# Tokens of the first two experts picked on TensorE instead of gathered by DMA

## The chip, the cores and the metric

The kernel runs on one core of a Trainium2 chip. The metric is the device time in microseconds (us) of one execution; lower is better.

## What is computed

A hybrid decoder layer over 512 tokens and 16 meta tokens: two attention groups, one output projection, and then a hierarchical mixture of experts. The part that matters here is the mixture: each token takes the best of 4 groups and the best 2 of the group's 8 experts, and each of the 32 experts is a SwiGLU of 1024 to 256 to 1024.

```python
u = rmsnorm(h, g_ffn).reshape(B * L, D)
group_logits = (u @ w_group + b_group)
g_idx = jnp.argmax(group_logits, axis=-1)
...
within = jnp.einsum('tg,tge->te', one_hot(g_idx, N_GROUPS), exp_logits)
top_v, top_i = lax.top_k(within, TOP_K)
...
for e in range(N_EXPERTS):
    hid = jax.nn.silu(u @ w1[e]) * (u @ w3[e])
    y = y + combine[:, e:e + 1] * (hid @ w2[e])
return h + y.reshape(B, L, D)
```

## The kernel before

All engines run their own instruction lists, written by hand in program order and tied by semaphores; no scheduler reorders them. The program has a projection stage, two attention sweeps (the second ends near 338 us of the span), an output projection with the router, and the expert loop, which begins near 383 us.

**Router and tables.** The 512 tokens are four tiles `x[:, i, :]` of 128 tokens by 1024 values in SBUF; after `add_mla` (L1462) a tile holds the residual h. For each tile in `TILE_ORDER` (3, 2, 1, 0; the last is `LAST`) PE turns it (L1947) and multiplies by the router's weights (L1959); DVE finds groups and experts (`choose_group`, `choose_experts`, L1482 to L1515) and writes `ehots`, one-hot over 32 experts for each of the two choices; PE counts each token's rank inside its expert (`ranks`, L1970 and L1971); and DVE (`positions`, L1531 to L1540) writes `slot_hot`, one-hot over the expert's 64 slots. `index` (L2130) multiplies `slot_hot` by `tok_hot` on PE and so gives, for each expert and slot, the number of the token in it. DVE turns that into `idx` (L1677), the list of an indirect DMA. A count of tokens for each expert (L2142, L1680, L1681) gives `over`, which is 1 when an expert has more than 64 tokens; a fallback then runs at the end. `keep_warm` (L1793) issues bf16 products whose result nobody reads.

**Expert loop.** ACT has stored each h tile to `h_rows` in DRAM (L1055). For each expert e, POOL issues an indirect DMA (L865) that gathers its rows from `h_rows` into `xg[e % 2]`, 64 rows of 1024 values; rows of empty slots are not written, and so `xg` was zeroed once before (L842). PE turns `xg` by 8 transposes (`turn_gathered`, L2149); DVE scales the result into `xt` (`dve_turned`, L1698); PE multiplies by w1 and w3 (`expand`, L2190); ACT scales rows and copies (L1226); PE turns the hidden rows (L2204); ACT and DVE form the gated product; PE multiplies by w2 (`contract`, L2219); ACT copies (L1248) and POOL scatters the rows to `y_rows` (L855) for the first 29 experts.

**Weights.** An expert's weights are 3 MB (w1, w3 and w2 of 1 MB each). SP issues all loads on one queue into a ring of 7 places. Experts 0 to 5 and w1 of expert 6 are loaded before the loop as memory comes free (the last of them, w1 and w3 of expert 4 and all of expert 5, at the end of the output projection); w3 of expert 6 (L654) waits for the first two gathers (`xg_in`), and its w2 (L675) for `tables_read`, early in the loop. From expert 7 on, w1 and w3 are issued (L660, L661) when `expand` of the expert 7 earlier has ended (`h13_done`) and w2 (L667) when its `contract` has ended. After the last expert the kernel reads `y_rows` back (L696), adds, and stores the output (L699).

## Time and profile before

| | us |
|---|---|
| median of 3 runs | 641.33 |
| lowest and highest | 639.18, 642.98 |
| the profiled execution's own time | 639.66 |
| its span, first to last instruction | 637.8 |
| mean granted TensorE clock | 0.972 of 2.4 GHz |

The profile is of one execution. The span is 1.9 us shorter than that execution's own time, which is 1.7 us under the median. A line such as L2190 is one of kernel.py. "PE" is matmul and "PEld" is the load of the stationary operand, which overlaps it. A float32 product with a stationary table of full width stands as two records, so that "x12" at L2279 are six products. In a timeline the first number is the start in us of the span, the second the length from the first record's start to the last one's end.

### The profile page before, as it was taken

Reading aid. Unit: us, or ns where it says so; the run is one execution under the profiler, and the core shown is the slowest. Engines: PE = TensorE matmul, PEld = TensorE weight load, DVE = VectorE, ACT = ScalarE, POOL = GpSimd, SP = SyncE. Lnnn points to the kernel's source line nnn. Section 1 sums busy time; section 2 is a strip of 40 time slices with the busy share of each in tenths; the row PEclk is TensorE's granted clock in tenths of the full one; section 3 lists DMA queues with packets and bytes.
Section 4 is the critical chain, followed back from the end, with each engine's and each line's share of the span. In section 5 each row is a group of like instructions: output and inputs, shape, how many; then the busy total and the mean of one; then the engine's idle time right before and its main releaser. Section 6 shows DMA issues by size and latency. Waiting matters only on the chain.

```text
span 637.8 us, 9266 instructions
## 1 busy us (share of the span) xinstructions
PE 601.4 (94%) x3595; PEld 412.1 (65%) x3595; DVE 246.5 (39%) x574; ACT 228.6 (36%) x434; POOL 137.9 (22%) x226
## 2 busy tenths in 40 slices
PE   8799999998999997999999989999999999877896
PEld 8588778895666564566788746665665665544554
DVE  3644254224553875287554741111111111101217
ACT  6726414343545353684525611212122122111220
POOL 8100001110133321133400011323323322122110
PEclk8799799999999998999999979999999999899999
DMA  8920000007000064000579488999999999999995
GB/s 251 388 77 1 0 2 0 1 1 282 0 2 0 23 242 141 1 1 1 228 288 409 161 326 292 380 380 393 397 382 391 387 387 394 396 384 400 398 384 209
DMA packets 32525, 139.97 MB, mean 219 GB/s; under 512 B 8681, under 2 KB 10777, under 8 KB 19425
## 3 DMA queue, kind: packets, MB, share of 16 engines
q1 hardware_dynamic: 25440, 124.92, 50.8%
q0 software_dynamic: 6464, 12.36, 5.8%
q10 hardware_dynamic: 576, 2.10, 0.8%
q8 instruction: 29, 0.48, 0.3%
q14 instruction: 16, 0.12, 0.1%
HBM read 131.28 MB, written 16.06 MB: 231 GB/s over the span
## 4 chain that ended last, share of the span: by engine, by line
PE 82%; DVE 10%; issue 3%; DMA 2%; ACT 2%; SPq 0%; DVEq 0%; ACTq 0%
PE ps L2190 18%; PE ps L1857 15%; PE ps L2219 9%; PE ps L2044 5%; PE ps L1933 5%; PE ps L1988 5%; PE ps L2149 5%; PE ps L2033 5%; PE ps L1793 3%; PE ps L2204 2%; DMA w_in_ffcq<-in_w_in 2%; PE ps L2008 2%; PE ps L1830 1%; PE ps L2083 1%; DVE sums_s L1607 1%
## 5 line engine op out<-in xcount | busy, mean ns | idle before, releaser
L2190 PE MATMUL ps<-w,xt 128*64 128x256 f32 x1024 | 118.1, 384 | 13.6 <-issue 12.8
L2190 PEld LDWEIGHTS ps<-w,xt 128*64 128x64 f32 x1024 | 77.5, 139 | 60.9 <-issue 31.9
L1698 DVE TENSOR_TENSOR xt<-ps,g_ffn_c 128x512 f32<-128x512 f32 x32 | 22.1, 691 | 198.7 <-PE ps L2149 198.7
L2219 PE MATMUL ps<-w,hT 128*64 128x512 f32 x256 | 61.8, 605 | 0.0
L1226 ACT ACTIVATE hsb<-ps,row_scale 128x256 f32<-128x256 f32 x32 | 15.1, 473 | 125.2 <-PE ps L2190 125.2
L865 POOL DMA_INDIRECT xg<-h_rows,idx x32 | 30.6, 956 | 113.5 <-PE ps L2149 106.7
L855 POOL DMA_INDIRECT y_rows<-yh,idy x29 | 29.4, 1012 | 64.2 <-ACT yh L1248 64.2
L791 POOL TENSOR_SCALAR_AFFINE_SELECT probT<-probT 128x128 f32<-128x128 f32 (+2 forms) x80 | 23.4, 310 | 90.4 <-ACT probT L1146 89.7
L2044 PE MATMUL ps<-probT,vals 128*128 128x512 f32 (+4 forms) x160 | 42.6, 411 | 0.0
L2033 PE MATMUL ps<-qT,kT 68*128 68x400 f32 (+9 forms) x160 | 42.1, 407 | 0.0
L2149 PEld LDWEIGHTS ps<-ident,xg 64*128 64x128 f32 x256 | 30.6, 200 | 12.4 <-issue 12.4
L1618 DVE TENSOR_REDUCE nmax<-ps 128x1 bf16<-128x528 f32 (+1 forms) x64 | 28.0, 502 | 25.3 <-PE ps L2009 25.3
L2033 PEld LDWEIGHTS ps<-qT,kT 68*128 68x128 f32 (+1 forms) x160 | 26.9, 190 | 14.2 <-issue 7.7
L2044 PEld LDWEIGHTS ps<-probT,vals 128*128 128x128 f32 x160 | 26.8, 191 | 13.9 <-issue 7.1
L1607 DVE RECIPROCAL sums_s<-sums_s 128x512 f32<-128x512 f32 x8 | 26.8, 3352 | 21.6 <-ACT mixT L1156 21.6
L2149 PE MATMUL ps<-ident,xg 64*128 64x64 f32 x256 | 35.0, 277 | 0.0
L1248 ACT ACTIVATE yh<-ps 128x512 f32<-128x512 f32 x29 | 17.3, 597 | 46.4 <-PE ps L2219 46.4
L2219 PEld LDWEIGHTS ps<-w,hT 128*64 128x64 f32 x256 | 15.6, 136 | 22.6 <-issue 18.8
L1146 ACT ACTIVATE probT<-ps 128x416 f32<-128x416 f32 (+1 forms) x48 | 25.1, 540 | 4.6 <-PE ps L2033 4.4
L1793 PE MATMUL ps<-onesb,identb 128*128 128x512 bf16 x91 | 25.5, 428 | 0.8 <-DVE over L1681 0.8
L768 POOL CAST kTb<-kT 68x1024 bf16<-68x1024 f32 (+1 forms) x5 | 4.4, 885 | 97.6 <-PE ps L1857 85.4
L1155 ACT ACTIVATE sums_s<-ps 64x512 f32<-64x512 f32 x16 | 9.5, 591 | 37.8 <-PE ps L2044 37.8
(333 smaller groups left out, 987.5 us busy)
## 6 DMA issues: line engine op xcount, KB each, us to landing
w<-in_w SPq DMA_DIRECT2D x96, 1024.0 KB, 28.4
y_rows<-zeros POOLq DMA_DIRECT2D x1, 4096.0 KB, 12.3
yg<-y_rows SPq DMA_DIRECT2D x4, 1024.0 KB, 11.6
x<-in_x SPq DMA_DIRECT2D x4, 512.0 KB, 5.6
w_in_v<-in_w_in SPq DMA_DIRECT2D x1, 2048.0 KB, 10.5
w_in_k<-in_w_in SPq DMA_DIRECT2D x1, 2048.0 KB, 16.2
w_in_q<-in_w_in SPq DMA_DIRECT2D x1, 2048.0 KB, 21.0
w_oa<-in_w_o SPq DMA_DIRECT2D x1, 2048.0 KB, 10.2
```

The costliest lines, as they stand in the source:

```text
L855: pool.indirect_dma_start(out=y_halves, out_offset=bass.IndirectOffsetOnAxis(ap=idy[:, e:e + 1].bitcast(U32), axis=0), in_=yh[e % 2][:, :] ...
L865: pool.indirect_dma_start(out=xg[e % 2][:, :, :].rearrange("p k n -> p (k n)"), out_offset=None, in_=h_rows, in_offset=bass.IndirectOffset ...
L1607: dve.reciprocal(sums_s[m % 2][:, :], sums_s[m % 2][:, :]).then_inc(sums_inv, 1)
L1793: pe.matmul(ps[:, bank, :], identb[:, :], onesb[:, :].unsqueeze(1).to_broadcast([P, 4, P]), start=True, stop=True)
L1857: ins = pe.matmul(ps[0:unit_rows(u), n % 4, 0:w], ua[:, k, unit_cols(u)], wa[b][:, k, 0:w], start=(k == 0 and p == 0), stop=(k == DK - 1 a ...
L1933: ins = pe.matmul(ps[:, bank + q, :], m[:, k, i * P:(i + 1) * P], w[:, k, q * 512:(q + 1) * 512], start=(n == 0 and k == 0), stop=(n == 2 ...
L1988: ins = pe.matmul(ps[:, b0 + j, 0:nn], src[:, k, block_cols(t) if kind == "kv" else cols(t)], w[:, k, j * nn:(j + 1) * nn], start=(k == 0) ...
L2033: ins = pe.matmul(ps[:, b, c0:c0 + wide], kT[0:depth(g), h, block_cols(j)], qT[0:depth(g), h, q0:], start=True, stop=True)
L2044: ins = pe.matmul(ps[:, OUT, q0:SEQ], value(j, g % H), probT[g % 2][:, b, c0:c0 + SEQ - q0], start=(j == 0), stop=(j == 3))
L2149: ins = pe.transpose(ps[:, b, k * slots:(k + 1) * slots], src[:, k::DK], ident[half, half])
L2190: ins = pe.matmul(ps[j * slots:(j + 1) * slots, 2 + b, 0:F], xt[b][:, k, :], w13[s][:, j, k, :], start=(k == 0), stop=(k == DK - 1))
L2219: ins = pe.matmul(ps[q * slots:(q + 1) * slots, 6 + b, :], hT[b][:, m, :], w2s[s][:, m, q * 512:(q + 1) * 512], start=(m == 0), stop=(m == ...
```

## The change

Experts 0 and 1 are no longer gathered by DMA. `first_slots` makes, for each token tile, a one-hot table of 128 tokens by 2 x 64 slots: `slot_hot` of both choices times `ehots` of experts 0 and 1, and the two choices added. POOL makes it for the first three tiles and DVE for the last. `first_tokens` multiplies each table (stationary) by the tile of h (moving, two halves of 512 columns) and sums over the four tiles in PSUM banks 0 and 1. ACT copies the one half and DVE the other into `xg_both`, the buffer that the gathers of experts 0 and 1 filled. The zeroing of `xg` goes, since every row is now written. The gathers begin with expert 2. Two `keep_warm` calls (10 and 26 products) go. `turn_gathered(1)` and `dve_turned(1)` move ahead of `expand(0)`; PE's wait for `over_made` moves to `turn_hidden(0)`, and DVE's work on `over` behind `dve_turned(1)`. SP no longer waits for the first two gathers ahead of L654's load. Some private semaphores are replaced by the engine's common step semaphore with the same waits.

```diff
+        def first_slots(eng, p):
+            i = TILE_ORDER[p]
+            eng.wait_ge(hot_made, p + 1)
+            if p:
+                eng.wait_ge(first_made, p)
+            eng.tensor_tensor(first_both[:, :, :].rearrange("p c (e s) -> p c e s", e=2),
+                              slot_hot[:, i, :, :].rearrange("p c (e s) -> p c e s", e=2),
+                              ehots[:, i, :, 0:2].unsqueeze(3).to_broadcast([P, 2, 2, slots]), ALU.mult
+                              ).then_inc(first_part, 1)
+            eng.wait_ge(first_part, p + 1)
+            eng.tensor_tensor(first_hot[:, i, :], first_both[:, 0, :], first_both[:, 1, :], ALU.add
+                              ).then_inc(first_made, 1)
@@ SP
-            for b in range(2):
-                sp.wait_ge(xg_in[b], 16)
             sp.dma_start(w13[6][:, 1, :, :], w3_v[6]).then_inc(w13_in[6], 16)
@@ POOL
-            pool.wait_ge(wo_done, 2 * NT)
-            pool.wait_ge(logits_done, NT)
-            pool.memset(xg_both[:, :, :], 0.0).then_inc(xg_blank, 1)
-            pool.wait_ge(xg_blank, 1)
+            for p in range(LAST):
+                first_slots(pool, p)
...
-            for e in range(NE):
-                if e >= 2:
-
-                    pool.wait_ge(xt_done, e - 1)
+            for e in range(2, NE):
+                pool.wait_ge(xt_done, e - 1)
@@ ACT
+            act.wait_ge(first_done, 1)
+            act.activation(first_half(0), ps[:, 0, :], ACT.Copy).then_inc(first_copied, 1)
@@ DVE
             positions(LAST)
+            first_slots(dve, LAST)
+            dve.wait_ge(first_done, 2)
+            dve.tensor_copy(first_half(1), ps[:, 1, :]).then_inc(first_copied, 1)
...
+            dve_turned(0)
+            dve_turned(1)
             dve.wait_ge(counted, 1)
@@ PE
+            def first_tokens(p):
+                i = TILE_ORDER[p]
+                pe.wait_ge(h_made, NT)
+                pe.wait_ge(first_made, p + 1)
+                for q in range(2):
+                    ins = pe.matmul(ps[:, q, :], first_hot[:, i, :], x[:, i, q * 512:(q + 1) * 512],
+                                    start=(p == 0), stop=(p == LAST))
+                    if p == LAST:
+                        ins.then_inc(first_done, 1)
...
-            for p in range(LAST):
-                index(p)
-            keep_warm(COUNT, 10)
+            index(0)
+            index(1)
+            first_tokens(0)
+            first_tokens(1)
             ranks(LAST)
+            first_tokens(2)
+            first_tokens(LAST)
+            index(2)
             index(LAST).then_inc(idx_done, 1)
...
-            pe.wait_ge(over_made, 1)
-            keep_warm(7, 26)
             turn_gathered(0)
+            turn_gathered(1)
             for e in range(NE):
                 expand(e)
-                if e < NE - 1:
+                if 1 <= e < NE - 1:
                     turn_gathered(e + 1)
```

On PE, between the router's last product and expert 1's, the kernel before issues these in a row (`x4` or the like is a count of equal ones; the names are those of the section on the kernel; lines are of the kernel before):

```order
L2130 MATMUL ps<-tok_hot,slot_hot 128x64
L1793 MATMUL ps<-onesb,identb 128x512 x10
L1970 MATMUL ps<-picks,onesb 128x32 [waits pos_made,picks_made]
L1970 MATMUL ps<-picks,onesb 128x32 x2
L1971 MATMUL ps<-picks,before 128x32
L2130 MATMUL ps<-tok_hot,slot_hot 128x64 [waits hot_made]
L2130 MATMUL ps<-tok_hot,slot_hot 128x64
L2142 MATMUL ps<-picks,onesb 128x32 x4
L1793 MATMUL ps<-onesb,identb 128x512 [waits over_made]
L1793 MATMUL ps<-onesb,identb 128x512 x25
L2149 MATMUL ps<-ident,xg 128x64 [waits xg_in0]
L2149 MATMUL ps<-ident,xg 128x64 x7
```

The changed kernel has, in the same place (L2146 is `index`, L2157 `first_tokens`, L1986 and L1987 `ranks`, L2173 the count, L2180 `turn_gathered`):

```order
L2157 MATMUL ps<-x,first_hot 128x512
L1986 MATMUL ps<-picks,onesb 128x32 [waits pos_made,picks_made]
L1986 MATMUL ps<-picks,onesb 128x32 x2
L1987 MATMUL ps<-picks,before 128x32
L2157 MATMUL ps<-x,first_hot 128x512 [waits first_made,h_made]
L2157 MATMUL ps<-x,first_hot 128x512
L2157 MATMUL ps<-x,first_hot 128x512 [waits first_made,h_made]
L2157 MATMUL ps<-x,first_hot 128x512
L2146 MATMUL ps<-tok_hot,slot_hot 128x64 [waits hot_made]
L2146 MATMUL ps<-tok_hot,slot_hot 128x64
L2146 MATMUL ps<-tok_hot,slot_hot 128x64 [waits hot_made]
L2146 MATMUL ps<-tok_hot,slot_hot 128x64
```

The ten and the 26 bf16 products are gone, four products of 512 columns stand behind the ranks (four more stand ahead of them), and the indices of the last two tiles stand behind those.

On DVE, behind the last tile's tables, the changed kernel has (L1697 is the copy of the second half, L1562 `dve_turned`):

```order
L1553 SCALAR_TENSOR_TENSOR pos_t<-ranks_all,esels 128x2
L602 TENSOR_TENSOR first_both<-slot_hot,ehots 128x256 [waits first_made,hot_made]
L607 TENSOR_TENSOR first_hot<-first_both 128x128 [waits first_part]
L1697 COPY xg<-ps 128x512 [waits first_done]
L1700 TENSOR_SCALAR idy<-ps,half_f 128x32 [waits idx_done]
L1702 TENSOR_SCALAR idx<-idy 64x32 [waits idy_made]
L1703 COPY row_scale<-ps 128x32
L1562 TENSOR_TENSOR xt_103<-ps,g_ffn_c 128x512 [waits xt_done]
L1562 TENSOR_TENSOR xt_104<-ps,g_ffn_c 128x512 [waits xt_done]
L1707 TENSOR_REDUCE most<-ps 128x1 [waits counted]
```

Two table operations and a copy now stand between `pos_t` and `idy`, and both scalings into `xt` ahead of the count's reduction.

## Rows read from the trace of the kernel before

**Rows 1.** Page, part 1: busy time, share of the span, instructions of each engine.

```profile
PE 601.4 (94%) x3595; PEld 412.1 (65%) x3595; DVE 246.5 (39%) x574; ACT 228.6 (36%) x434; POOL 137.9 (22%) x226
```

**Rows 2.** Windows: length, busy PE, PEld, DVE, ACT, POOL; clock, DMA share, GB/s.

```profile
362.60:378.00 15.40, 12.38 (x75) 7.53 (x74) 11.26 (x62) 5.45 (x11) 2.97 (x3) 0.84 0.94 365
378.00:392.00 14.00, 13.15 (x89) 8.39 (x88) 1.83 (x4) 2.03 (x3) 1.86 (x2) 0.93 0.59 187
392.00:608.00 216.00, 203.66 (x1484) 123.76 (x1480) 30.75 (x70) 40.24 (x89) 57.86 (x60) 0.99 1.02 390
```

**Rows 3.** Timeline of PE, expert products: start, length, names, idle before, releaser.

```profile
398.41 3.62 PE L2190 MATMUL ps<-w,xt 128*64 128x256 f32 x32
405.19 3.62 PE L2190 MATMUL ps<-w,xt 128*64 128x256 f32 x32
...
544.15 5.20 PE L2190 MATMUL ps<-w,xt 128*64 128x256 f32 x32 [2.64 <-issue]
...
605.24 3.67 PE L2190 MATMUL ps<-w,xt 128*64 128x256 f32 x32 [0.99 <-issue]
...
613.24 3.67 PE L2190 MATMUL ps<-w,xt 128*64 128x256 f32 x32 [0.41 <-issue]
```

**Rows 4.** Waits of the SP queue, 320 to 638: total us, times, longest.

```profile
SPq L653 <- DMA xg<-h_rows,idx: 17.1, 1, 17.1
```

**Rows 5.** Timeline of the SP queue, two weight loads at the hand-over.

```profile
382.31 0.33 SPq L654 DMA_DIRECT2D w<-in_w  x1
388.55 0.33 SPq L660 DMA_DIRECT2D w<-in_w  x1
```

**Rows 6.** Timeline of all engines from the router's end to expert 0's product.

```profile
367.25 1.53 PE L2130 MATMUL ps<-tok_hot,slot_hot 128*128 128x64 f32 x12
...
371.40 0.24 PE L1970 MATMUL ps<-picks,onesb 128*128 128x32 bf16 x3 [0.46 <-DVE picks L1511]
...
372.61 0.15 DVE L1540 SCALAR_TENSOR_TENSOR pos_t<-ranks_all,esels 128x2 int32<-128x2 f32 x1
...
373.27 0.31 PE L2142 MATMUL ps<-picks,onesb 128*128 128x32 bf16 x4
...
374.41 8.54 PE L1793 MATMUL ps<-onesb,identb 128*128 128x512 bf16 x26 [0.83 <-DVE over L1681]
...
374.99 1.05 POOL L865 DMA_INDIRECT xg<-h_rows,idx  x1 [6.49 <-DMA h_rows<-x]
...
382.89 1.09 PE L2149 MATMUL ps<-ident,xg 64*128 64x64 f32 x8
...
384.09 0.69 DVE L1698 TENSOR_TENSOR xt<-ps,g_ffn_c 128x512 f32<-128x512 f32 x1 [8.07 <-PE ps L2149]
...
384.83 3.67 PE L2190 MATMUL ps<-w,xt 128*64 128x256 f32 x32 [0.85 <-DVE xt L1698]
```

**Rows 7.** Timeline of PE near the end: six products of 512 columns.

```profile
627.19 5.42 PE L2279 MATMUL ps<-yg,coef_diag 128*128 128x512 f32 x12
```

**Rows 8.** Groups by line and shape: count, busy, mean ns, idle before.

```profile
L1597 DVE TENSOR_TENSOR rope_g<-st_mla,gr_q 128x256 f32<-128x256 f32 x4 | 1.7, 424 | 0.1
L1547 DVE TENSOR_TENSOR rope_t<-rope_g,rope_cs 128x128 f32<-128x128 f32 x4 | 1.1, 284 | 0.0
...
L1248 ACT ACTIVATE yh<-ps 128x512 f32<-128x512 f32 x29 | 17.3, 597 | 46.4 <-PE ps L2219 46.4
...
L835 POOL TENSOR_TENSOR w_route<-w_route,g_ffn_r 128x288 f32<-128x288 f32 x1 | 0.7, 662 | 7.3 <-DMA w_route<-in_w_expert 7.3
```

**Rows 9.** DMA queues, 320 to 638: gathers and scatters, packets, MB, share.

```profile
q0 software_dynamic: 4880, 8.02, 7.7%
```

**Rows 10.** Windows of one microsecond around the fall and return of the clock.

```profile
373.00:374.00 1.00, 0.58 (x8) 0.48 (x7) 0.45 (x4) 0.00 (x0) 0.00 (x0) 0.60 0.95 397
...
380.00:381.00 1.00, 1.00 (x6) 0.48 (x5) 0.00 (x0) 0.00 (x0) 0.00 (x0) 0.98 0.11 37
```

**Rows 11.** Line L1548 on DVE: min, median, max ns, starts, shapes.

```profile
L1548 DVE TENSOR_TENSOR rope_t<-rope_g,rope_cs x4: 283/285/1123, 209.1 to 245.1; 128x128 f32<-128x128 f32 x4
```

More of the change, by code:

```diff
@@ L1028, in _ @@
                     act.wait_ge(ff_in, 1)
-                    act.activation(ff_e[:, :, :], ff[:, :, :], ACT.Abs).then_inc(ff_abs, 1)
-                    act.wait_ge(ff_abs, 1)
-                    act.activation(ff_e[:, :, :], ff_e[:, :, :], ACT.Exp, scale=-1.0).then_inc(ff_exp, 1)
-                    act.wait_ge(ff_exp, 1)
+                    step(act.activation(ff_e[:, :, :], ff[:, :, :], ACT.Abs))
+                    step(act.activation(ff_e[:, :, :], ff_e[:, :, :], ACT.Exp, scale=-1.0))
                     act.activation(ff_e[:, :, :], ff_e[:, :, :], ACT.Ln, bias=1.0).then_inc(ff_log, 1)
@@ L2169, in turn_gathered @@
                 b = e % 2
-                pe.wait_ge(xg_in[b], 16 * (e // 2 + 1))
-                if e >= 2:
+                if e < 2:
+                    pe.wait_ge(first_copied, 2)
+                else:
+                    pe.wait_ge(xg_in[b], 16 * (e // 2))
                     pe.wait_ge(xt_out, e - 1)
```

50 lines of the change are left out of this document (26 added, 24 removed).

## The prediction

> **What bounds the kernel now.** I read the busy times first. PE is busy 94% of the span [rows 1], which would make it the bound, but a modelled busy PE says nothing of who waits for whom, so I went on to windows by stage and to the timeline of the expert loop. From 392 to 608 us the DMA share is 1.02, at 390 GB/s [rows 2]. Expert products first come every 6.78 us (398.41, 405.19), back to back; from 544 on they begin behind idle time that no engine's work ends (2.64, 0.99, 0.41 us), and come every 8.0 us (605.24, 613.24) [rows 3]. "issue" there means that no semaphore of an engine ended the wait, and the only other thing that `expand` waits for is its weights. So the loop has two regimes. PE goes through the seven experts held in the ring faster than the queue refills it, and when the lead is used up the queue sets the pace to the end. In bytes: 25 experts of 3.15 MB from expert 7 on, and w2 of expert 6, are 79.7 MB; at 390 GB/s that alone is 204 of the 216 us, and gathers and scatters fill the rest. **The end is therefore set by when the queue begins to run without a break**, and the question is what it does before that.
>
> Between 378 and 392 its share is 0.59, though it was 0.94 from 362.6 to 378 [rows 2]: 0.41 x 14 = 5.7 us idle. The SP queue shows why. It waited 17.1 us for the first two gathers [rows 4], issued one load of 1 MB at 382.31, and could issue expert 7's only at 388.55 [rows 5], when `expand(0)` had ended and freed a place. The end thus hangs on the end of `expand(0)`, and this hangs on a serial piece: tables, indices, gather, turn, scale, product. The gather is issued at 374.99, and PE, filled with 26 bf16 products from 374.41, begins to turn only at 382.89; the product starts at 384.83 [rows 6].
>
> **What the change takes away.** The gather's 7.9 us between issue and turn, the 26 products and the 10 before them. SP issues the last 1 MB some 17 us earlier. The zeroing of `xg` lay in POOL's idle time and is worth nothing.
>
> **What it adds, along the path.** A product of a full table with 512 columns costs 5.42 / 6 = 0.90 us, from the nearest row of the same kind [rows 7].
> 1. PE ends the router and begins `index` at 367.25; 12 records took 1.53 us [rows 6], so the 8 of two tiles take 1.0: 368.25. Then four products, 3.6 us: 371.85. Before, the 10 warm products and a wait of 0.46 us lay here, and `ranks(LAST)` began at 371.40. It is now 0.45 us late.
> 2. DVE's `positions(LAST)` ended at 372.76 [rows 6]; now 373.2. It makes the last table itself: 128x256 at 0.42, 128x128 at 0.28 us [rows 8], and two hand-offs that I put at 0.05 each: 374.0. PE meanwhile does tile 2's two products, 372.1 to 373.9, under cover.
> 3. The last tile's two products: 374.0 to 375.8. ACT copies the first half (0.60 us [rows 8]) from 374.9 on, hidden; DVE copies the second in at most the 0.69 us of a 128x512 operation out of PSUM [rows 6]: 376.5. PE in that time does the last two indices (1.0) and the count (0.31 [rows 6]) and is free at 377.1. So the copies cost nothing, but if they took over 1.3 us, each further tenth would be a tenth late.
> 4. `turn_gathered(0)` and `(1)`, 1.09 us each with their tails [rows 6], some 2.1 together: 379.2. DVE's scaling of expert 0 ends at 377.1 + 1.09 + 0.11 + 0.69 = 379.0, under the second turn. `expand(0)` starts at **379.2 against 384.83, 5.7 us earlier**. It takes 3.67 in both, so `h13_done` and expert 7's load come at about 382.9.
>
> Behind it, `turn_hidden(0)` no longer has the second turn ahead of it and waits about half a us for ACT, but expert 1's product still comes some 5.9 us earlier than it did. `over` is due only there and is ready by about 380.5. The gather of expert 2, now POOL's first, is issued when the first turn ends (378.2) and wanted at the end of `expand(1)`, about 389; before, 7.9 us lay between issue and use, so 11 is enough. The gather of expert 3 has 16.
>
> **What of this reaches the end.** All, if the queue is free when expert 7's load comes. Its earlier work grows by the 1 MB issued earlier, about 2.5 us at the rate of rows 2, and shrinks by two gathers. It ran dry near 380 before (share 0.11 in 380 to 381 [rows 10]) and does so near 381.5 now, ahead of 382.9, so no part of the 5.7 us is eaten. 3 us of idle queue stay. On the other side the queue gains a little: gathers 2 and 3 both fall into the dry piece, where before only one fell into the stretch ahead of expert 7. All 61 gathers and scatters took 7.7% of 318 us [rows 9], 0.40 us each, so 0.4 us less.
>
> **The tables on POOL.** The first two lie beside work with slack. The third starts when `slot_hot` of tile 2 is ready, near 366.7, and is wanted at 372.1. POOL's nearest row is 0.66 us for 128x288 [rows 8]; two operations are about 1.0, so there is cover for five times that. But DVE is then on the path (`weigh`, then the last `choose_group`). DVE and POOL can hold each other up: one 128x128 operation of DVE took 1.12 us where its like take 0.28 [rows 11]. Bounds: nothing, or both POOL operations, 1.0 us. I take 0.3, nearer to nothing, since the median of such operations shows no delay.
>
> The Trainium skill (SBUF, "SBUF: two separate sides") says that the pair of ports shared by VectorE and GpSimd is an exclusive lock, held for a whole instruction, for which a VectorE operation with two SBUF inputs also contends. The longest of rows 11 agrees with it. By that rule the upper bound would be the value, and the time 0.7 us higher.
>
> **Sum:** 5.7 + 0.4 - 0.3 = 5.8 us. From the profiled execution's 639.66 that is 633.9, and from the median, which stands 1.7 us above it, 641.33 - 5.8 = **635.5**. Its own range: the table products at 0.85 to 1.2 us each (six of the eight lie on the path, -0.3 to +1.8), DVE's delay 0 to 1.0: 634.0 to 638.0.
>
> **Rivals.**
>
> *The clock falls at the same place as before (chance 0.13).* The granted clock is 0.60 in 373 to 374, half (1.2 GHz) behind it and 0.98 only in 380 to 381 [rows 10]. It fell while PE mostly waited (0.58 us busy in that window), and again near 544 after 2.64 us idle, where `expand` took 5.20 instead of 3.62 [rows 3]. If it falls at 374 all the same and stays for the same 6.5 us, half of that, 3.2 us, is lost: 638.7. Against it: from 367.25 to 382.9 PE now has no gap above 0.2 us, and it is fed with float32 products. For it: the 36 warm products are gone, and PE depends on three other engines keeping time.
>
> The Trainium skill (TensorE: Matmul & The Clock Gate, "Part 1: The HAM clock gate") says that the throttled state is the default and activity releases it. That rule counts the real products as activity like the warm ones, and the return to 0.98 under the 26 products agrees [rows 10]. It would take this rival only if a table came late.
>
> *Slower (0.09): half clock through `expand(0)`.* PE's work from 374.0 to 382.9 is then done at 1.2 GHz and takes twice 8.9 us. `h13_done` comes at 391.8, 3.3 us later than before, less 0.4: 644.2. It decides from 12.2 us at half clock (twice 5.7 + 0.4) on. What speaks for it is that nothing is left that would warm PE if it fell; against it, that 26 products brought the clock back in 6 us before, and the work here is as dense.
>
> *The start isn't what the end hangs on (0.06).* If the queue's mean rate sank in step, say because gathers and weights meet otherwise, only the 0.4 us would be left: 640.9. Against it stands the share of 1.02 in all of 216 us. The same number would come out if the tables weren't ready in time, that is if `first_tokens(LAST)` began near 379.7.
>
> **How the numbers follow.** The forecast's case has 0.72, the others 0.13, 0.09 and 0.06. The forecast is the likeliest case. The range of 8 in 10 takes its own range and the first rival: 633.0 to 639.2, the lower end one us below the case's own, for the drift between executions (639.18 to 642.98 before). A measurement of this kernel can tell about 0.5%, 3.2 us, from no change. Faster by more than that is the forecast's case, 0.71; within it are the clock's fall, the lost link and the edge of the main case, 0.20; slower by more needs most of the third case, 0.09.
>
> **What the profile of the changed kernel would show.** The first product of a table near 368.3 and the last one's end near 375.8; `expand(0)` at 379.2; expert 7's load on SP at about 382.9, 5.7 us earlier than before; a DMA share of about 0.75 between 378 and 386 and about 1.0 from there on; granted clock 1.00 from 368 to 390. At the end, expert 31's product still behind a short wait for weights, near 607. I would be wrong by step 2 if POOL or DVE delay the last table, by step 3 if PE stands at its wait for `first_copied`, by the clock if a window around 374 to 383 shows half, and by the main argument if `expand(0)` moves by 5 us and `expand(31)` does not.

## The result, and the profile after

The changed kernel takes **632.47 us** (median of 4 executions, 632.39 to 635.71); the kernel before, run beside it, 641.0 (639.18 to 642.98). The ratio is 0.9865 (0.9835 to 0.9896): 8.5 us faster, where 5.8 were forecast. The direction and the place were right; the time lies half a microsecond below the range. The profiled execution took 632.39 us, with a span of 630.7 us, against 639.66 and 637.8.

The page's busy times and the windows of the kernel after; these answer to [rows 1] and [rows 2]. Columns of the windows: length, busy PE, PEld, DVE, ACT, POOL; clock, DMA share, GB/s.

```profile
PE 599.2 (95%) x3575; PEld 412.6 (65%) x3575; DVE 249.2 (40%) x577; ACT 229.2 (36%) x435; POOL 138.8 (22%) x229
...
362.60:378.00 15.40, 14.50 (x86) 9.13 (x85) 11.39 (x55) 5.79 (x12) 1.07 (x2) 1.00 0.96 373
378.00:392.00 14.00, 13.14 (x107) 8.72 (x108) 4.21 (x17) 2.81 (x6) 2.97 (x3) 1.00 0.88 341
392.00:608.00 216.00, 203.86 (x1480) 124.23 (x1478) 31.51 (x71) 41.44 (x91) 57.10 (x59) 0.99 1.01 388
```

The busy times say almost nothing: PE was 94% busy and is 95% busy. The second window says it: the DMA share between 378 and 392 went from 0.59 to 0.88, that is 0.29 x 14 = 4.1 us of idle queue less. The clock in it went from 0.93 to 1.00.

Timeline of the SP queue of the kernel after, the last load ahead of the hand-over and expert 7's; it answers to [rows 5]:

```profile
364.93 0.49 SPq L672 DMA_DIRECT2D w<-in_w  x1
382.28 0.33 SPq L678 DMA_DIRECT2D w<-in_w  x1
```

The load that hung on the gathers is issued 17.4 us earlier, and expert 7's 6.3 us earlier. Timeline of the kernel after, all engines, from the third table on POOL to expert 1's product and expert 2's turn; it answers to [rows 6]:

```profile
366.43 0.62 POOL L602 TENSOR_TENSOR first_both<-slot_hot,ehots 128x256 f32<-128x256 f32 x1 [7.27 <-DVE slot_hot L1549]
366.52 0.54 DVE L1536 TENSOR_TENSOR wt<-wt 128x1 f32<-128x1 f32 x1
...
367.10 0.16 DVE L1537 RECIPROCAL coef<-wt 128x1 f32<-128x1 f32 x1
367.13 0.45 POOL L607 TENSOR_TENSOR first_hot<-first_both 128x128 f32<-128x128 f32 x1
367.30 0.30 DVE L1538 TENSOR_TENSOR coef<-coef,wt 128x1 f32<-128x1 f32 x1
...
367.89 3.65 PE L2157 MATMUL ps<-x,first_hot 128*128 128x512 f32 x8
...
371.64 0.24 PE L1986 MATMUL ps<-picks,onesb 128*128 128x32 bf16 x3
...
373.43 0.29 DVE L607 TENSOR_TENSOR first_hot<-first_both 128x128 f32<-128x128 f32 x1
...
373.87 1.95 PE L2157 MATMUL ps<-x,first_hot 128*128 128x512 f32 x4 [0.15 <-DVE first_hot L607]
...
375.00 0.60 ACT L1231 ACTIVATE xg<-ps 128x512 f32<-128x512 f32 x1 [4.63 <-PE ps L2157]
...
375.66 1.00 PE L2146 MATMUL ps<-tok_hot,slot_hot 128*128 128x64 f32 x8
...
375.86 0.69 DVE L1697 COPY xg<-ps 128x512 f32<-128x512 f32 x1 [2.14 <-PE ps L2157]
...
376.70 1.58 PE L2180 MATMUL ps<-ident,xg 64*128 64x64 f32 x16
...
378.56 3.67 PE L2222 MATMUL ps<-w,xt 128*64 128x256 f32 x32 [0.28 <-DVE xt L1562]
...
384.93 3.67 PE L2222 MATMUL ps<-w,xt 128*64 128x256 f32 x32
...
388.53 1.09 PE L2180 MATMUL ps<-ident,xg 64*128 64x64 f32 x8
```

Every step is where it was forecast, in that order, and each within 0.65 us. Expert 0's product starts at 378.56 instead of 384.83. The last expert's product, forecast near 607, comes at 606.13 with the same short wait for weights as in [rows 3], and the two gathers that are gone show as 160 packets less than in [rows 9] (PE's timeline; DMA queues from 320 us to the end):

```profile
606.13 3.67 PE L2222 MATMUL ps<-w,xt 128*64 128x256 f32 x32 [0.42 <-issue]
```

```profile
q0 software_dynamic: 4720, 7.59, 7.4%
```

**One cut for all profiles.** Absolute positions shift between executions of one kernel by several us, long before the change's place. So I cut every profile at three events: the *mark*, the first weight load that SP issues behind the output projection (362.57 before, 362.29 after); expert 7's load; and expert 31's product. From mark to expert 7's load is the *hand-over*, from there to expert 31's product the *stream*. What follows is the tail, 24.5 to 24.6 us in every copy. Before, the hand-over took 388.55 - 362.57 = 25.98 and the stream 224.69. After, they took 19.99 and 223.85. With the mark's 0.28 that is 5.99 + 0.84 + 0.28 = 7.1 us, the whole difference of the spans.

### The profile page after: what moved, and what is told of

Read it like the earlier page. It is cut to its first block, busy times and chain, and to the rows that moved or that the text cites. A ratio compares the mean times of both kernels' runs of the same rounds, so it can differ in the third digit from the quotient of the medians.

```text
span 630.7 us, 9237 instructions
## 1 busy us (share of the span) xinstructions
PE 599.2 (95%) x3575; PEld 412.6 (65%) x3575; DVE 249.2 (40%) x577; ACT 229.2 (36%) x435; POOL 138.8 (22%) x229
## 4 chain that ended last, share of the span: by engine, by line
PE 81%; DVE 10%; issue 3%; DMA 2%; ACT 2%; SPq 0%; DVEq 0%; ACTq 0%
PE ps L2222 18%; PE ps L1873 15%; PE ps L2253 9%; PE ps L2060 6%; PE ps L1949 5%; PE ps L2004 5%; PE ps L2180 5%; PE ps L2049 5%; PE ps L2238 2%; DMA w_in_ffcq<-in_w_in 2%; PE ps L2024 2%; PE ps L1846 1%; PE ps L1809 1%; PE ps L2099 1%; DVE sums_s L1630 1%
## 5 line engine op out<-in xcount | busy, mean ns | idle before, releaser
L1562 DVE TENSOR_TENSOR xt<-ps,g_ffn_c 128x512 f32<-128x512 f32 x32 | 22.0, 691 | 185.9 <-PE ps L2180 185.9
L879 POOL DMA_INDIRECT xg<-h_rows,idx x30 | 28.8, 961 | 108.9 <-PE ps L2180 108.6
L2180 PEld LDWEIGHTS ps<-ident,xg 64*128 64x128 f32 x256 | 30.2, 200 | 11.6 <-issue 11.5
L2180 PE MATMUL ps<-ident,xg 64*128 64x64 f32 x256 | 34.4, 277 | 0.0
L2024 PE MATMUL ps<-kTb,qTb 68*128 68x512 bf16 (+9 forms) x80 | 16.7, 296 | 5.2 <-ACT mix_root L1060 2.6
```

The costliest lines, as they stand in the source:

```text
L879: pool.indirect_dma_start(out=xg[e % 2][:, :, :].rearrange("p k n -> p (k n)"), out_offset=None, in_=h_rows, in_offset=bass.IndirectOffset ...
L2024: pe.matmul(to[:, c0:c1], q, kTb[0:depth(g), h, c0:c1], start=True, stop=False)
L2180: ins = pe.transpose(ps[:, b, k * slots:(k + 1) * slots], src[:, k::DK], ident[half, half])
```

## The experiments

My theory in all of them: the end hangs one for one on when expert 7's load is issued, and the change wins by issuing it earlier. Times stand beside runs of the kernel before on the same chip. Names with b_ are variants of the kernel before, those with a_ of the changed kernel; b_same, b_same2, a_same and a_same2 are unaltered copies, each profiled again. "e7 load" is the issue time of expert 7's load.

| kernel | mark | e7 load | hand-over | stream | median us (executions) | ratio to before |
|---|---|---|---|---|---|---|
| before | 362.57 | 388.55 | 25.98 | 224.69 | 641.0 (4) | |
| b_same | 365.79 | 391.77 | 25.98 | 225.09 | 642.45 (12) | 0.9994 (0.9966 to 1.0022) |
| b_same2 | 361.46 | 387.76 | 26.30 | 225.30 | 641.34 (12) | 0.9986 (0.9960 to 1.0013) |
| b_steps | 361.18 | 387.17 | 25.99 | 225.50 | 640.71 (12) | 0.9988 (0.9964 to 1.0013) |
| b_steps2 | 364.23 | 389.07 | 24.84 | 224.90 | 640.77 (12) | 0.9986 (0.9966 to 1.0005) |
| b_no26 | 363.39 | 390.38 | 26.99 | 224.46 | 641.53 (12) | 0.9985 (0.9960 to 1.0010) |
| b_free_load | 363.99 | 392.86 | 28.87 | 224.53 | 641.87 (12) | 1.0009 (0.9989 to 1.0029) |
| after | 362.29 | 382.28 | 19.99 | 223.85 | 632.47 (4) | 0.9865 (0.9835 to 0.9896) |
| a_same | 361.41 | 381.40 | 19.99 | 224.42 | 632.45 (6) | 0.9870 (0.9848 to 0.9893) |
| a_same2 | 365.52 | 385.51 | 19.99 | 223.66 | 633.82 (5) | 0.9873 (0.9844 to 0.9903) |
| a_late_load | 361.44 | 381.43 | 19.99 | 223.25 | 633.41 (6) | 0.9884 (0.9866 to 0.9902) |
| a_warm26 | 362.51 | 388.13 | 25.62 | 223.78 | 639.09 (10) | 0.9963 (0.9941 to 0.9985) |
| a_old_turn | 364.15 | 384.14 | 19.99 | 226.26 | 636.66 (6) | 0.9934 (0.9912 to 0.9957) |
| a_load_behind | 363.19 | 383.55 | 20.36 | 225.88 | 636.44 (5) | 0.9906 (0.9871 to 0.9941) |
| a_direct | 362.68 | 388.63 | 25.95 | 225.19 | 641.21 (12) | 1.0010 (0.9990 to 1.0029) |
| a_direct2 | 363.49 | 381.74 | 18.25 | 227.29 | 634.15 (6) | 0.9853 (0.9818 to 0.9888) |
| a_less | 360.99 | 380.98 | 19.99 | 220.63 | 630.07 (4) | 0.9829 (0.9807 to 0.9851) |

### a_warm26: the changed kernel, held up by 26 products

```diff
+            keep_warm(7, 26)
             turn_gathered(0)
             turn_gathered(1)
```

> The changed kernel with the 26 bf16 products put back ahead of the first turn, so that everything from there on starts later by their length, about 5.9 us at the full clock (10 of them took 2.32 us). Theory 1 (the end hangs on the start of expert 7's load, one for one): 632.5 + 5.9 - what the copies' wait hides (0.1) = about 638.3 us, with expert 7's load near 388.1. Rival (the gain is made in the stream: two gathers fewer and the 1 MB load issued early): within 1 us of 632.5.

Measured 639.09 us, 6.6 above the changed kernel. Timelines of PE and of the SP queue in its profile:

```profile
376.83 5.77 PE L1809 MATMUL ps<-onesb,identb 128*128 128x512 bf16 x26
...
382.53 1.59 PE L2180 MATMUL ps<-ident,xg 64*128 64x64 f32 x16
```

```profile
388.13 0.33 SPq L678 DMA_DIRECT2D w<-in_w  x1
```

The 26 products take 5.77 us at full clock and stand on the path by intent. Expert 7's load comes 5.6 us later behind the mark, and the stream is as short as in the changed kernel (223.78). So a delay of the hand-over passes to the end whole, 225 us later. The median moved by 6.6 us, 1.0 more than the hand-over; the other pieces of one profile differ by as much between equal kernels. This is the run on which the main argument rests: everything else of the change is still in this kernel, and 6.6 of its gain of 8.6 us are gone.

### a_load_behind and a_less: is it the queue that paces the stream?

```diff
@@ a_load_behind
             load_expert(5, 5)
+            sp.wait_ge(h13_done, 1)
             sp.dma_start(w13[6][:, 1, :, :], w3_v[6]).then_inc(w13_in[6], 16)
@@ a_less
                 sp.wait_ge(h13_done, e - RING + 1)
+                if e == 20:
+                    sp.dma_start(w13[s][:, 0, 0:1, :], w1_v[e][:, 0:1, :]).then_inc(w13_in[s], 16)
+                    sp.dma_start(w13[s][:, 1, 0:1, :], w3_v[e][:, 0:1, :]).then_inc(w13_in[s], 16)
+                    return
```

> The changed kernel with w3 of expert 6 (1 MB) issued behind expert 0's product, right ahead of expert 7's loads, instead of 17 us earlier. Theory 1 (from expert 7's load on the queue never rests, so each MB that is put behind that point costs its time): 1.05 MB / 0.39 = 2.7 us slower, 635.2 us. Rival (PE's pace of 6.78 us an expert bounds the loop, and the queue has slack): within 0.5 us of 632.5.

> The changed kernel with 7 of 8 chunks of w1 and w3 of expert 20 left out of their loads (expert 20 computes with stale weights in them): 1.84 MB less on the queue, the same work on PE. Theory 1 (the queue paces the end): 1.84 / 0.39 = 4.7 us faster, 627.8, and expert 31's product 219.4 us behind expert 7's load instead of 224.1. Rival (PE or another engine paces the end and the waits seen are harmless): within 0.5 us of 632.5.

a_load_behind takes 1 MB from ahead of the queue's idle piece and puts it where the queue begins to run without a break, in front of expert 7's load. Timeline of its SP queue:

```profile
383.17 0.33 SPq L673 DMA_DIRECT2D w<-in_w  x1
383.55 0.43 SPq L679 DMA_DIRECT2D w<-in_w  x1
```

The moved load stands at 383.17, 19.98 us behind the mark, just where expert 7's stood in the changed kernel, and expert 7's follows it. From 383.17 to expert 31's product are 226.26 us, 2.4 more than the changed kernel's 223.85, and it took 636.44 us. The 1.05 MB at 388 GB/s are 2.7 us. So bytes behind the start cost about their full time on the queue; ahead of it, where the queue still ran dry before expert 7's load, the same bytes cost nothing that shows.

a_less takes bytes out of the stream: it leaves out the loads of 7 of the 8 chunks of w1 and w3 of expert 20, and expert 20 computes with what lay in their place. The stream was 3.2 us shorter (220.63), not 4.7, and the median 630.07 against 633.41 of a_late_load on the same chip, with the profiled execution at 627.88. Timeline of PE of a_less, the products of experts 30 and 31:

```profile
593.91 3.67 PE L2226 MATMUL ps<-w,xt 128*64 128x256 f32 x32 [0.99 <-issue]
601.61 3.67 PE L2226 MATMUL ps<-w,xt 128*64 128x256 f32 x32
```

The last product no longer waits for its weights (in the changed kernel it did, 0.42 us), so at the very end PE's own work takes over. That accounts for little of what is missing from the 4.7 us: expert 30's product, which still waits 0.99 us for weights, starts 593.91 - 380.98 = 212.9 us behind expert 7's load, in the changed kernel 598.12 - 382.28 = 215.8, so it too is only 2.9 us earlier. Where the other 1.8 us went isn't shown. Fewer bytes made the stream shorter, as the theory says, but by two thirds of their time on the queue.

### a_late_load and b_free_load: was the freed load a cause of its own?

```diff
@@ a_late_load (on the changed kernel)
             load_expert(5, 5)
+            sp.wait_ge(first_copied, 2)
             sp.dma_start(w13[6][:, 1, :, :], w3_v[6]).then_inc(w13_in[6], 16)
@@ b_free_load (on the kernel before)
-            for b in range(2):
-                sp.wait_ge(xg_in[b], 16)
             sp.dma_start(w13[6][:, 1, :, :], w3_v[6]).then_inc(w13_in[6], 16)
```

> The changed kernel with the 1 MB load of expert 6 held back until both halves of the picked tokens are copied (376.5 instead of 364.9 us). The queue is busy until about 380 in either case, so by theory 1 nothing moves: the piece to expert 7's load stays 19.99 us, and the end behind it within 0.4 us: 632.5. Rival (issuing it early is part of the gain): 1 to 2.5 us slower. By theory P of the run above the median may still lie up to 2 us higher with the same pieces in the profile, through a later start of the hand-over.

> The kernel before with only SP's wait for the first two gathers removed, so that the 1 MB load of expert 6 is issued at about 365 instead of 382.3. Theory 1 (that load fell into an empty queue and was done before expert 7's load came): no gain, the piece to expert 7's load stays 25.98 us or grows by up to 1 us, since the load now delays the gathers: 641 to 642. Rival: 1 to 2.5 us faster.

a_late_load issues the 1 MB at 375.74 instead of 364.93. Hand-over 19.99, stream 223.25, 633.41 us against 632.45 and 633.82 of the unaltered copies: no difference. The early load is no part of the gain.

b_free_load gives the kernel before that same early load. It gained nothing (641.87 against 641.68 beside it). Windows and PE's timeline of b_free_load:

```profile
380.00:382.00 2.00, 1.56 (x8) 0.49 (x5) 0.00 (x0) 0.00 (x0) 0.00 (x0) 1.00 1.02 375
382.00:384.00 2.00, 0.00 (x0) 0.00 (x0) 0.00 (x0) 0.00 (x0) 0.00 (x0) 1.00 0.91 266
384.00:386.00 2.00, 1.11 (x8) 0.95 (x8) 0.00 (x0) 0.00 (x0) 0.00 (x0) 0.68 0.10 35
386.00:388.00 2.00, 1.15 (x7) 0.77 (x8) 0.69 (x1) 0.00 (x0) 0.94 (x1) 0.50 0.00 0
```

```profile
384.89 1.11 PE L2147 MATMUL ps<-ident,xg 64*128 64x64 f32 x8 [3.33 <-DMA xg<-h_rows,idx]
...
386.86 5.96 PE L2188 MATMUL ps<-w,xt 128*64 128x256 f32 x32 [0.85 <-DVE xt L1696]
```

With 1 MB more on the queue the gather lands later, PE sits idle for 3.33 us behind its 26 products, the clock drops to 0.50, and expert 0's product takes 5.96 us instead of 3.67: the hand-over is 28.87 us in this profile. In this profile the early load did get in the gathers' way. The median didn't move, and the profiled execution (643.79 us) stands 1.9 above it, so this is what can happen, not what the wait was worth on the whole.

### b_no26: were the 26 warm products the bound before?

```diff
             pe.wait_ge(over_made, 1)
-            keep_warm(7, 26)
             turn_gathered(0)
```

> The kernel before without the 26 bf16 products ahead of the first turn, and nothing else changed. They ended at 382.95, and the first two gathers had both landed by 382.3. Theory 1 (the gather sets the start; the products are cover, and keep the clock): PE idles from 374 to about 382, the turn starts 0 to 1 us earlier, but expert 0's product runs at 1.2 GHz for most or all of its length, 2 to 3.6 us longer: 0.5 to 3 us slower than before, 641.5 to 644. Rival (the products were the bound, and the clock is back at once): 0.6 to 1.5 us faster, 639.5 to 640.5. The clock in 382 to 390 tells them apart.

641.53 us against 642.28 beside it: no difference that can be told. Timeline of PE of b_no26:

```profile
382.86 1.11 PE L2149 MATMUL ps<-ident,xg 64*128 64x64 f32 x8 [8.54 <-DMA xg<-h_rows,idx]
...
384.83 5.51 PE L2190 MATMUL ps<-w,xt 128*64 128x256 f32 x32 [0.85 <-DVE xt L1698]
```

The turn now waits for the gather itself. Against the mark the product starts 0.8 us earlier (21.44 instead of 22.26) and takes 1.84 us longer, at half clock. So in the kernel before two things ended almost together: the gather, and 26 products that took 8.54 us at half clock. Taking away the products alone gave nothing, and a_warm26, which has the products and no gather, stands only 2.0 us under the kernel before (639.09 against 641.08). A copy of the kernel before shows the other outcome; timeline of PE of b_same2:

```profile
373.24 5.79 PE L1793 MATMUL ps<-onesb,identb 128*128 128x512 bf16 x26 [0.84 <-DVE over L1681]
...
380.73 1.07 PE L2149 MATMUL ps<-ident,xg 64*128 64x64 f32 x8 [1.70 <-DMA xg<-h_rows,idx]
...
382.65 5.07 PE L2190 MATMUL ps<-w,xt 128*64 128x256 f32 x32 [0.85 <-DVE xt L1698]
```

Here the clock was full through the warm products; they ended early, PE waited 1.70 us, and the clock fell during the product instead. The hand-over was 26.30. In b_steps2 the clock was down from 376 only to about 379, and the hand-over was 24.84. In the changed kernel neither the gather nor the clock has a part in it, and four profiles of its hand-over agree to 0.01 us.

### a_old_turn: must the second turn move ahead too?

```diff
             turn_gathered(0)
-            turn_gathered(1)
             for e in range(NE):
                 expand(e)
-                if 1 <= e < NE - 1:
+                if e < NE - 1:
                     turn_gathered(e + 1)
                 turn_hidden(e)
```

> The changed kernel with the turn of expert 1 behind expert 0's product again, as before the change; DVE's list is unchanged. Theory (the start of expert 0's product hangs on the scaling of expert 0 alone, and the second turn lies under it): product at 378.6 as in the changed kernel, time within 0.3 us of 632.5. Rival (moving the turn is part of the gain): 1 us slower, since the turn then lies between expert 0's and expert 1's products; and DVE's later work behind its second scaling comes 4 us later, which could hold back the slot coefficients and with them w2 of expert 6.

636.66 us, 4.2 above the changed kernel. I had taken this order for neutral. Timeline of all engines of a_old_turn, and one of its windows:

```profile
384.03 1.09 PE L2180 MATMUL ps<-ident,xg 64*128 64x64 f32 x8
...
385.99 0.15 DVE L1708 TENSOR_SCALAR over<-most 128x1 int32<-128x1 f32 x1
...
386.29 0.47 PE L2238 MATMUL ps<-ident,hsb 128*128 128x128 f32 x2 [1.16 <-DVE over L1708]
...
388.96 5.36 PE L2222 MATMUL ps<-w,xt 128*64 128x256 f32 x32
```

```profile
390.00:392.00 2.00, 2.00 (x12) 1.19 (x10) 0.00 (x0) 0.00 (x0) 0.00 (x0) 0.50 0.99 336
```

DVE's list still had the second scaling ahead of `over`. With the second turn behind `expand(0)`, `over` waits for it too, and PE, which needs `over` ahead of `turn_hidden(0)`, stands 1.16 us. The clock then falls to 0.50, and expert 1's product takes 5.36 us. Expert 8's load is issued at 394.36; in the changed kernel at 388.64, which against the marks is 3.9 us. The queue has a gap (share 0.44 in 394 to 396), and the stream is 2.4 us longer. What this shows is narrow: with DVE's list as it is, the turn has to go ahead. It also shows how thin the cover is: a wait of 1.2 us at this place, with the half clock behind it, costs the stream 2.4. (The mark of this profile is 1.9 us late besides, which is scatter.)

### a_direct and a_direct2: no buffer and no turn

Both let the table move and hold the tile of h, so that the tokens come out turned, and scale them from PSUM. The copies and both turns go.

```diff
-                for q in range(2):
-                    ins = pe.matmul(ps[:, q, :], first_hot[:, i, :], x[:, i, q * 512:(q + 1) * 512],
+                for k in range(DK):
+                    ins = pe.matmul(pair(0, D)[:, k * P:(k + 1) * P], x[:, i, k::DK], first_hot[:, i, :],
```

In a_direct2 the stationary columns are contiguous, `x[:, i, k * P:(k + 1) * P]`, and w1, w3 and the gain of experts 0 and 1 are loaded in that order.

> The changed kernel with the picks made the other way round: the residual tile's columns are stationary (8 strided chunks of 128), the one-hot table of 128 slots moves, and PE writes the tokens already turned. The copies by ACT and DVE and both turns go; DVE scales straight from PSUM. Theory 1: 8 products of 128 columns cost about what 2 of 512 do (16 records of 0.114 us, 1.8 us a tile), the scaling ends at 376.5 and expert 0's product starts behind the count at about 376.8 instead of 378.56: expert 7's load 1.8 us earlier, at 380.5, whose first bytes (2.4 us later) still find the queue almost empty: 630.7 us. Rival (the queue isn't empty by then: its share was 1.04 in 378 to 380 and 0.67 in 380 to 382): half or less of it, 631.6 to 632.5. Rival 2 (strided stationary loads are slow, 0.38 us a product and more): 3 us a tile and more, at or above 632.5.

> As the direct variant, in which 16 products with strided stationary columns took 7.87 us (0.49 us each, 0.246 a record), but with contiguous stationary columns: w1 and w3 of experts 0 and 1 are loaded with rows in the order k, p instead of p, k (rows of 1 KB instead of 8 KB), and their gains come in the same order. Theory 1: a record with a contiguous table takes 0.114 us as in the index products, 1.8 us a tile; expert 0's product at 376.8 against 378.56, expert 7's load 1.8 us earlier and the queue empty by then: 630.7 us. Rival 1 (the queue isn't empty by then): 631.6 to 632.5. Rival 2 (loads of a stationary operand bound a stream of 128-column products whatever the stride, about 0.19 us a record): 3.0 us a tile; two tiles ahead of the last ranks and two behind make it 2.4 us later than in theory 1 each: 633 to 635.

Timelines of PE, 16 products in either: first a_direct, then a_direct2.

```profile
368.28 7.87 PE L2155 MATMUL ps<-first_hot,x 128*128 128x128 f32 x32
...
384.84 3.67 PE L2217 MATMUL ps<-w,xt 128*64 128x256 f32 x32
```

```profile
369.09 3.79 PE L2158 MATMUL ps<-first_hot,x 128*128 128x128 f32 x32
...
377.95 3.67 PE L2220 MATMUL ps<-w,xt 128*64 128x256 f32 x32
...
384.70 5.00 PE L2220 MATMUL ps<-w,xt 128*64 128x256 f32 x32
```

A stationary operand read with a step of 32 bytes costs 7.87 / 32 = 0.246 us a record, a contiguous one 3.79 / 32 = 0.118. a_direct took 641.21 us. Its hand-over is back at 25.95 and the gain is gone, the second witness for the main argument. a_direct2 differs from it in the step, and in the order of loading that goes with it, and has a hand-over of 18.25. The Trainium skill (SBUF — State Buffer, "Door 1: The DMA port swizzle") has a rule on this: reads that cross into a new line of 16 bytes at each element pay a penalty. A step of 32 bytes is such a read, and the two runs agree.

That hand-over is as expected, 1.7 us shorter than the changed kernel's, and yet a_direct2 took 634.15, no less than the copies of the changed kernel; its ratio, 0.9853 (0.9818 to 0.9888), leaves room for anything between all of the 1.7 us and none. In its profile, which is of the slowest of its six executions (635.32), the stream is longer instead (227.29). There the DMA share is 0.98 in 380 to 382, so expert 7's load, at 381.74, met a queue that was still busy; and the clock fell in 384 to 386, expert 1's product took 5.00 us, and expert 8's load came only at 389.74. I didn't separate the two, nor what the other order of loading does to the queue. That the hand-over's gain ends about here, because a load issued earlier only stands in line behind the queue's own earlier work, is likely and not shown.

### b_steps, b_steps2 and the copies: the semaphores, and the scatter

The change also replaces five private semaphores by the engines' step semaphores. b_steps and b_steps2 are the kernel before with that part alone.

```diff
-                    act.activation(ff_e[:, :, :], ff[:, :, :], ACT.Abs).then_inc(ff_abs, 1)
-                    act.wait_ge(ff_abs, 1)
+                    step(act.activation(ff_e[:, :, :], ff[:, :, :], ACT.Abs))
```

> The kernel before with only the replacement of private semaphores by the engines' step semaphores (the same waits in the same places). Two profiles each show that the change shortens the piece from the first weight load behind the output projection to expert 7's load by 5.99 us and the rest by about 0.75, 6.7 in all, and 8.6 us are measured. The missing 1.9 us lie ahead, where only these semaphores differ. Theory S (the semaphores are worth it): 1.5 to 2 us faster than before, that load at 361.5 to 362.5 us in the profile. Theory P (programs with equal work ahead scatter by such amounts, for a reason that the lists don't show): within 1 us of before on either side.

> The kernel before with the semaphores alone replaced, again. Theory S (they are worth the remaining 1.3 us): 1 to 1.5 us under the kernel before on the same chip, in the median of both groups together 1.0 or more. Theory P (equal programs ahead of the hand-over, scatter alone): within 0.5 us of the kernel before.

> The kernel before, unaltered, for a second profile of it. The first profile (span 637.8 us) lies 1.4 us under the median of 23 further executions (641.08 against its 639.66), and it is open where an execution at the median loses these 1.4 us. Theory A: ahead of the hand-over, in the attention stages, where the last weight load behind the output projection was issued at 363.6 to 365.5 us in the profiles so far; then the pieces behind are as long as in the first profile: 24.7 us from that issue to expert 7's load, 224.7 us from there to expert 31's product. Theory B: in the hand-over itself, through a longer stretch at half clock: that piece is 26 us or more in an execution near the median. Theory C: in the expert loop, 226 us or more.

> The kernel before again, for a third profile and to see how far the medians of one and the same program lie apart. By both theories the pieces are 25.98 us to expert 7's load and 224.5 to 225.5 from there to expert 31's product; by theory P the medians of equal programs differ by 0.5 to 1 us, which is most of the remainder.

> The changed kernel unaltered, as a base for the others of this group and to see how executions scatter. Theory 1 (the whole gain is the earlier issue of expert 7's load, 6.3 us, and 0.8 us of a shorter stream behind it; the rest of the measured 8.5 us is that the profiled execution of the kernel before stood 1.3 us under its own median): the changed kernel stays at 632.4 to 632.6 us in most executions, the kernel before scatters over 639 to 643, and the difference of medians is 7 to 9 us. Rival (the 8.5 us are a steady difference and the traces miss 1.3 us of it): profiles of the kernel before taken again give spans of 639 us and more as often as 637.8.

> The changed kernel again, for a third profile. Pieces: 19.99 us and 223.3 to 224.4. By theory S the first weight load behind the output projection is again at 361.4 to 362.3; by theory P it may as well be at 363 to 364, with a median of 632 to 634.

Over both runs, the 24 executions have a mean of 640.6 us, the two unaltered copies of the kernel before 641.6 (24 executions). Each ratio's interval holds 1. The means suggest up to 1 us, but by their means the two unaltered copies also stood 0.5 and 0.7 under the runs beside them. Whether the semaphores are worth anything from 0 to 1 us stays open.

The copies settle another point. Over all runs of this case 97 executions of the kernel before have a mean of 641.8 us (637.4 to 647.4), and 15 of the changed kernel 633.2 (631.8 to 635.7). The mean difference is 8.6 us, so the gain isn't a lucky draw. No run isolates the 10 warm products ahead of the ranks or the zeroing of `xg`; both went in every variant of the changed kernel.

## Why the prediction was right in kind and short in size

**The step that failed** is the size of the sum, not its mechanism: the term that lifts the profiled execution to the median, put at 1.7 us and measured at 0.1, and the hand-over, put at 5.4 us with the term for DVE and measured at 5.99. The first is the larger, and it's a matter of drawing executions. There is bad luck in it too: of the changed kernel's 15 executions the mean is 633.2, and the copy a_same2 has a median of 633.82, both inside the range that 632.47 misses by half a us.

**Where the 3 us between 635.5 and 632.47 are.** The prediction made its sum for the profiled execution (633.9) and then added the 1.7 us by which the profile before stood under the median. Measured were 632.39 and a median 0.1 above that. So 1.5 us are terms of the sum, and 1.6 us are the step from profile to median. The terms are taken one by one below; 0.2 us of the 1.5 is that the execution's own time stands 1.9 us above the span before and 1.7 after.

*The step to the median (1.6 us).* It was taken as the same for both kernels. It isn't a property of the kernel: the profiled execution is one draw of executions that lie between 637.4 and 647.4. The mark alone lies anywhere from 361.0 to 365.8 in the profiles of the table, whose kernels differ ahead of it only in the five semaphores, a_direct2's order of loading and two tables on POOL. Before, the profile was a low draw (639.66, with a mean of 641.8 over 97 executions); after, both the profile (632.39) and the median of its four executions (632.47) lie 0.7 to 0.8 under the mean of 15.

*The hand-over (0.6 us).* Forecast 5.7 - 0.3 = 5.4, measured 5.99 between the two profiles. (By the prediction's own start times, 384.83 - 379.2, the 5.7 is 5.6.) Against the mark, expert 0's product was due 379.2 - 362.57 + 0.3 = 16.9 us behind it, and came 16.27 behind.
- Step 1 and the term for the tables on POOL: I charged 0.45 us because the ranks stand behind four products, and 0.3 us because DVE is held up, as a sum. They run beside each other. The four products were through at 367.89 + 3.65 = 371.54, the ranks' data came at 371.64, and DVE alone set that time: 0.52 us later against the mark than before, instead of 0.75.
- Step 2 held: last table made at 373.72, 11.43 us behind the mark, against 11.4 forecast without the 0.3. Step 3's copies cost nothing, as written: ACT 0.60, DVE 0.69 us, under the two indices and the count. The rest of step 3 was 0.1 us too long: I added whole lengths (1.0 and 0.31) where the next group starts 0.84 and 0.20 us behind the start of the one before, 0.27 us less, and left out the 0.15 us between the last table and its products.
- Step 4: the two turns took 1.58 us together, not 2.1. Product 0 then waited 0.28 us for DVE's scaling, which I had put under the second turn. Together this piece was 0.24 us shorter than forecast.

*The stream (0.4 us).* Forecast 0.4 for one gather less, measured 0.84 in these two profiles. Over the copies it is 225.10 (five profiles, before and b_steps among them) to 223.80 (four), 1.3 us. What makes it more than forecast isn't shown, nor that all of it belongs to the change: a_direct, with the same two gathers gone, has a stream of 225.19. The dry piece of the queue may take in more of the gathers and scatters than I counted, but no run isolates it.

*The mark (0.3 us)* is within the scatter, with the semaphores' open 0 to 1 us in it. Of the 8.6 us between the means, 5.8 are the hand-over over the same five and four profiles (25.82 to 19.99) and 1.3 the stream; the last 1.5 lie ahead of the mark or are scatter of the marks, and stay open.

**What held.** *What bounds the kernel*: the end follows expert 7's load one for one, shown by a_warm26 (+5.6 us of hand-over, +6.6 in the median) and by a_direct. *No part of the gain is eaten*: the queue was running dry when expert 7's load was issued at 382.28, and a_load_behind shows what the same bytes cost behind it. Windows of the kernel after:

```profile
380.00:382.00 2.00, 2.00 (x22) 1.20 (x18) 0.92 (x6) 0.00 (x0) 0.97 (x1) 1.00 0.67 211
382.00:384.00 2.00, 1.42 (x15) 1.19 (x11) 0.00 (x0) 1.70 (x2) 0.00 (x0) 1.00 0.46 84
```

*The freed load isn't a term*: a_late_load. *Expert 2's gather has cover enough*: expert 2's turn, at 388.53, shows no wait for it.

**Smaller slips that the forecast doesn't hang on.** The first wait for weights before was not near 544 but at 534.50 (0.32 us). The moved 1.05 MB are 2.7 us at 390 GB/s, not 2.5. And the lower end of the main case, by its own terms, is 635.5 - 0.3 - 0.3 = 634.9, not 634.0; the upper end, 638.0, is right.

**The contention of DVE and POOL** is clearer than the prediction had it. In the timeline after, DVE's L1536 (128x1, two inputs in SBUF) begins at 366.52 and ends at 367.06, just when POOL's L602 does (367.05); L1538 ends at 367.60, POOL's L607 at 367.58; the reciprocal between them, with one input, takes its usual 0.16 us. Instances of this line on DVE: min, median, max ns, starts, shapes; the kernel before first, then after.

```profile
L1523 DVE TENSOR_TENSOR wt<-wt x4: 158/159/159, 348.6 to 374.5; 128x1 f32<-128x1 f32 x4
```

```profile
L1536 DVE TENSOR_TENSOR wt<-wt x4: 159/544/545, 348.4 to 379.5; 128x1 f32<-128x1 f32 x4
```

Three of four meet a table and take 0.54 us. The rule of the Trainium skill that the prediction cites (SBUF — State Buffer, "SBUF: two separate sides"), an exclusive lock, is what these rows show. The price that I derived from it was the wrong one: the path loses what is left of POOL's instruction when a two-input operation meets it, less the operation's own 0.16 us. Here that is 0.38 and 0.14 us, and not the sum of POOL's instructions (1.07). My 0.3 was the better number and 0.52 the true one.

**The rivals.** *The clock falls at the same place*: it didn't. Windows of the kernel after, answering to [rows 10]:

```profile
373.00:374.00 1.00, 0.85 (x3) 0.16 (x2) 0.69 (x3) 0.00 (x0) 0.00 (x0) 1.00 0.97 410
380.00:381.00 1.00, 1.00 (x14) 0.64 (x12) 0.86 (x6) 0.00 (x0) 0.89 (x1) 1.00 0.85 266
```

It is 1.00 from 363 to 392, with no warm product behind 363.4; a_old_turn, where PE stands 1.16 us some 6 us later, shows that the threat was real. *Half clock through `expand(0)`*: not here, though b_no26 (5.51) and b_free_load (5.96) show it in the kernel before. *The start isn't what the end hangs on*: refuted by a_warm26.

**The range** was too narrow below. Its lower end left one us for the drift between executions, where the runs of before already lay 3.8 us apart, and took every unknown of the sum as a possible loss and hardly any as a gain.

## What to carry to other kernels

Where a ring of buffers runs ahead of its consumer and the transfer queue is then busy to the end, look for the instruction whose end releases the first of those transfers; here the microseconds taken off the serial piece ahead of it reached the end whole, and bytes ahead of it cost nothing that showed as long as the queue still ran dry before it. Just behind that point the cover was thin: a wait of 1.2 us there cost 4.2 us of the median. Before replacing one thing there, find what ends beside it: here taking away the warm products alone gave nothing, because the gather ended with them. In a sum of steps, two delays that meet at one wait count as the longer one, and a profile of one execution carries the scatter of everything ahead of it, so take differences between two events close to the change.

## What the runs showed of the hardware that I had not expected

- A VectorE operation of 128x1 with two SBUF inputs lasted until the GpSimd operation it met ended: 0.54 us instead of 0.16, three times of three (tables at 348.28, 358.02 and 366.43), while the reciprocal behind it kept its 0.16.
- Float32 products of 128 columns took 0.246 us a record with a stationary operand read in steps of 32 bytes (a_direct), 0.118 with a contiguous one (a_direct2).
- The turns of two experts that lie on partitions 0 to 63 and 64 to 127 took 1.58 us together, 16 products, where 8 alone took 1.09.
- The clock fell in every profile of the kernel before in the hand-over, but at different moments: in b_same within 376 to 377, behind 3 us in which PE was busy for 1.46, to return in 383 to 384; in b_same2 only in 382 to 386. It stayed at 1.00 there in all four profiles of the changed kernel (after, a_same, a_same2, a_late_load).
- Executions of one program with the same lists scatter over 10 us (637.4 to 647.4). In the three profiles of the kernel before the spans differ by 3.8 us (637.6 to 641.4) and the marks by 4.3, so there the scatter lies ahead of the stage that the change touches.
